# A hybrid decoder step: the last MLP unit by column groups, projection weights reloaded earlier, norm sums moved by one tile

## The reference

```python
h = rms_norm(x, norm_mix)
u = h @ w_in                        # RWKV-7 inputs, attention q/k/v/f, two merge gates
o_r, new_shift, new_wkv = rwkv_time_mix(u_r, ...)      # token shift, delta-rule state
o_f = attend(q, k, v, lf)                              # softmax with forget bias
merged = sigmoid(g_r) * (o_r @ w_br_rwkv) + sigmoid(g_f) * (o_f @ w_br_fox)
x = x + merged @ w_out
h2 = rms_norm(x, norm_ffn)
x = x + square(relu(h2 @ w_ffn_up)) @ w_ffn_down
y = rms_norm(x, norm_final)         # the outputs y_prompt and y_sample
```

## Time and profile before

| | us |
|---|---|
| median of 3 timed runs | 2189.82 |
| lowest and highest of them | 2179.16 and 2191.62 |
| the profiled execution | 2182.38 |
| its span, first to last instruction | 2180.6 |
| TensorE busy in it | 2074.7 (95%) |
| VectorE, ScalarE, GpSimd busy | 908.8, 594.1, 197.1 |
| mean granted TensorE clock | 0.986 |

### The profile page before, as it was taken

One profiled execution on the slowest core, in us unless ns is written; L12 is line 12 of the kernel. 1 busy time (PEld: TensorE's weight loads), 2 busy tenths in 40 slices (PEclk: granted clock), 3 DMA queues, 4 the chain that ended last, 5 costly groups with the idle time before them and its releaser, 6 DMA issues.

```text
span 2180.6 us, 42563 instructions
## 1 busy us (share of the span) xinstructions
PE 2074.7 (95%) x17388; PEld 1796.7 (82%) x17388; DVE 908.8 (42%) x1449; ACT 594.1 (27%) x956; POOL 197.1 (9%) x188
## 2 busy tenths in 40 slices
PE   7998899999999999998899999999999999999995
PEld 6996577777777777555566899999999999999995
DVE  6456543334444433514687654432223223222333
ACT  4014322222222222313445552332022112102212
POOL 0000112222222122001110000000000000000000
PEclk9999999999999999999999999999999999999998
DMA  3123610111121210765646461111111111111111
GB/s 145 48 78 113 214 39 22 44 44 49 49 58 49 67 42 25 184 134 188 204 150 227 147 230 63 48 43 45 48 48 39 49 48 38 48 48 40 46 38 79
DMA packets 105121, 180.96 MB, mean 83 GB/s; under 512 B 59951, under 2 KB 60271, under 8 KB 103431
## 3 DMA queue, kind: packets, MB, share of 16 engines
q1 hardware_dynamic: 102694, 170.65, 24.4%
q10 hardware_dynamic: 2304, 8.50, 1.6%
HBM read 145.58 MB, written 33.54 MB: 82 GB/s over the span
## 4 chain that ended last, share of the span: by engine, by line
PE 68%; issue 18%; POOL 4%; DVE 3%; DMA 3%; SPq 2%; ACT 2%; ACTq 0%; POOLq 0%; DVEq 0%
PE ps L289 40%; PE ps L369 13%; PE ps L941 3%; POOL arena L2113 3%; PE ps L942 3%; DMA weights<-in_wu 1%; SPq L758 1%; DMA normed<-in_vp 1%; PE ps L1123 1%; DVE arena L1893 1%; DMA normed<-in_kp 1%; PE ps L1060 1%; DVE arena L1912 1%; PE ps L1257 1%; PE ps L1182 1%
## 5 line engine op out<-in xcount | busy, mean ns | idle before, releaser
L369 PE MATMUL ps<-normed,weights 128*128 128x350 f32 x1344 | 429.9, 468 | 1.0 <-DVE arena L1686 1.0
L369 PEld LDWEIGHTS ps<-normed,weights 128*128 128x128 f32 x1344 | 246.0, 190 | 127.3 <-issue 6.8
L289 PE MATMUL ps<-h_high,wb_split 128*128 128x350 f32 x1536 | 290.5, 324 | 0.0
L289 PE MATMUL ps<-ff_high,wb_split 128*128 128x350 f32 x1536 | 290.0, 323 | 0.0
L299 ACT CAST wb_split<-weights 128x1024 fp32r<-128x1024 f32 x88 | 92.1, 1047 | 599.0 <-PE ps L289 590.9
L289 PEld LDWEIGHTS ps<-ff_high,wb_split 128*128 128x128 f32 x1536 | 255.2, 189 | 0.0
L289 PEld LDWEIGHTS ps<-h_high,wb_split 128*128 128x128 f32 x1536 | 254.7, 189 | 0.4
L2051 DVE TENSOR_TENSOR arena<-arena,ps 128x1050 f32 (+1 forms) x40 | 49.9, 1248 | 321.7 <-PE ps L289 321.7
L2113 POOL TENSOR_TENSOR arena<-arena,constants 64x512 f32<-64x512 f32 x120 | 132.5, 1104 | 406.4 <-DVE arena L1743 344.9
L941 PEld LDWEIGHTS ps<-arena 64*64 64x64 f32 x2400 | 145.0, 135 | 26.5 <-issue 26.1
L289 PE MATMUL ps<-ff_low,wb_split 128*128 128x350 f32 x768 | 165.5, 323 | 0.0
(11 more groups left out here) (291 smaller groups left out, 2895.2 us busy)
## 6 DMA issues: line engine op xcount, KB each, us to landing
weights<-in_wu SPq DMA_DIRECT2D x122, 512.0 KB, 3.5
normed<-in_vp SPq DMA_DIRECT2D x64, 260.0 KB, 4.6
normed<-in_kp SPq DMA_DIRECT2D x64, 256.0 KB, 5.4
arena<-chunk_dram SPq DMA_DIRECT2D x10, 1248.0 KB, 6.9
arena<-gate_dram SPq DMA_DIRECT2D x16, 525.0 KB, 3.9
chunk_dram<-arena SPq DMA_DIRECT2D x12, 520.0 KB, 4.0
chunk_dram<-fox SPq DMA_DIRECT2D x12, 520.0 KB, 3.8
arena<-samp_dram SPq DMA_DIRECT2D x10, 512.0 KB, 10.9
```

What stands on the lines that cost most here:

```text
L289: last = pe.matmul(PS[:, 3 * s + g, 0:G], ws[s][wh][:, k * P:(k + 1) * P], tile_of(x[xh], k)[:, g * G:(g + 1) * G], start=(k == 0 and wh + ...
L369: last = self.pe.matmul(PS[:, 6 + m % 2, 0:G], W[:, s, k * P:(k + 1) * P], HT[:, k, g * G:(g + 1) * G], start=(k == 0), stop=(k == KT - 1))
```

## The change

Four edits, all in the order of work:

1. `load_pairs` (pairs 1 to 7, input projection) waits for the split of the weights that it overwrites, in place of the end of the unit that uses them.
2. The norm sums of norm 0 are issued at tile 6 instead of tile 7: groups 0 and 1 before unit 1's half of tile 6, group 2 behind it.
3. The last unit (pair `PAIRS - 1`, slot 1) is run one column group after the other, 24 matmuls each into one bank, and everything behind it is per group: the add (`end_add`), the square (`end_square`), the sum in two matmuls (the running sum of seven squares, and the eighth square: `pe_end_sum`), Ln, Exp, and the multiply by gain and scale for 8 tiles (`end_normed`). Group 2's matmuls are issued in two halves between the sums.
4. GpSimd and the gain scaling on ScalarE have no part in the end; VectorE multiplies all 8 tiles, 350 columns at a time. SyncE stores twelve pieces, two tiles of one group each (128 x 2 rows of 1400 bytes).

```diff
             def load_pairs(v0, v1):
                 with sp.Fori(v0, v1) as v:
-                    load_w(v, 0)
-                    load_w(v, 1)
+                    for s in range(2):
+                        sp.wait_ge(w_split[s], v)
+                        load_w(v, s, wait=False)
...
-            for k in (0, 1, 6, 2, 3, 7, 4, 5):
-                if k < N_DVE:
-                    sp.wait_ge(h_ready, 2 * KT + k + 1)
-                else:
-                    sp.wait_ge(out_made, k - N_DVE + 1)
-                sp.dma_start(A["o_y"][:, k, :], HT[:, k, :]).then_inc(out_stored, 16)
+            for g in range(NG):
+                for j in range(KT // 2):
+                    sp.wait_ge(out_made, KT * g + 2 * j + 2)
+                    sp.dma_start(A["o_y"][:, 2 * j:2 * j + 2, g * G:(g + 1) * G],
+                                 HT[:, 2 * j:2 * j + 2, g * G:(g + 1) * G]).then_inc(out_stored, 16)
...
                 first_tile(k, 0)
-                if k == KT - 1:
+                if k == KT - 2:
                     pe.wait_ge(consts_in, 64)
                     pe_norm(pe, 0, (0, 1))
                 first_tile(k, 1)
-            pe_norm(pe, 0, (2,))
+                if k == KT - 2:
+                    pe_norm(pe, 0, (2,))
...
+            pe_down(FF_CH - 1, KT // 2 - 1)
+            pe_unit_split(pe, PAIRS - 1, 0, FS, of=BRO)
+
+            def pe_end(g, k0, k1):
+                ws = WSB[1]
+                for k in range(k0, k1):
+                    for wh, xh in ((0, 0), (0, 1), (1, 0)):
+                        last = pe.matmul(PS[:, NG + g, 0:G], ws[wh][:, k * P:(k + 1) * P],
+                                         FS[xh][:, k, g * G:(g + 1) * G], start=(k == 0 and wh + xh == 0),
+                                         stop=(k == KT - 1 and wh == 1))
+                if k1 == KT:
+                    last.then_inc(end_done, 1)
+
+            def pe_end_sum(g):
+                pe.wait_ge(sq_added, 3 * KT - 1)
+                at = slice(g * G, (g + 1) * G)
+                pe.matmul(PS[:, g, 0:G], ones, norms[2][1][:, at], start=True, stop=False)
+                pe.wait_ge(end_squared, g + 1)
+                pe.matmul(PS[:, g, 0:G], ones, norms[2][0][:, 1, at], start=False, stop=True)\
+                  .then_inc(ssum_ready[2], 1)
+
+            pe.wait_ge(w_split[1], PAIRS - PV_FILL)
+            pe.wait_ge(evac[1], PAIRS - 1 - PV_FILL)
+            pe_end(0, 0, KT)
+            pe_end(1, 0, KT)
             pe.wait_ge(evac[0], PAIRS - PV_FILL)
-            pe_norm(pe, 2)
+            pe_end_sum(0)
+            pe_end(2, 0, KT // 2)
+            pe_end_sum(1)
+            pe_end(2, KT // 2, KT)
+            pe_end_sum(2)
...
+            def end_square(g):
+                act.wait_ge(end_added, g + 1)
+                act.activation(sums[:, g * G:(g + 1) * G], XT[:, KT - 1, g * G:(g + 1) * G], ACT.Square)\
+                   .then_inc(end_squared, 1)
...
+            end_square(0)
+            end_square(1)
+            end_log(0)
+            end_exp(0, 1)
+            end_log(1)
+            end_square(2)
+            end_exp(1, 3)
+            end_log(2)
+            end_exp(2, 5)
...
-            dve_rms(dve, 2)
-            for k in range(N_DVE):
-                normed(dve, 2, k, V_NL, HT[:, k, :]).then_inc(h_ready, 1)
+
+            def end_add(g):
+                part = XT[:, KT - 1, g * G:(g + 1) * G]
+                dve.wait_ge(end_done, g + 1)
+                dve.tensor_tensor(part, part, PS[:, NG + g, 0:G], ALU.add).then_inc(end_added, 1)
+
+            def end_normed(g, count, tiles):
+                at = slice(g * G, (g + 1) * G)
+                dve.wait_ge(rms_ready[2], count)
+                for k in tiles:
+                    if k == KT - 1:
+                        dve.wait_ge(end_added, g + 1)
+                    dve.scalar_tensor_tensor(HT[:, k, at], XT[:, k, at], par[:, V_NL + k:V_NL + k + 1],
+                                             norms[2][2][:, at], ALU.mult, ALU.mult).then_inc(out_made, 1)
+
+            end_add(0)
+            end_add(1)
+            end_normed(0, 2, range(KT // 2))
+            end_add(2)
+            end_normed(0, 2, range(KT // 2, KT))
+            end_normed(1, 4, range(KT))
+            end_normed(2, 6, range(KT))
...
-            pool.wait_ge(rms_ready[2], NG + 1)
-            for k in range(N_DVE, KT):
-                pool.wait_ge(out_scaled, k - N_DVE + 1)
-                pool.tensor_tensor(HT[:, k, :], XT[:, k, :], norms[2][2], ALU.mult).then_inc(out_made, 1)
```

More of the change, by code:

```diff
@@ L58 @@
 RW_T = 14
-N_DVE = 6
 SCALE = HD ** -0.5
@@ L236, in build @@
         w_hi, w_split = [sem("w_hi0"), sem("w_hi1")], [sem("w_split0"), sem("w_split1")]
-        h_hi, out_scaled, out_made = sem("h_hi"), sem("out_scaled"), sem("out_made")
+        h_hi, out_made = sem("h_hi"), sem("out_made")
+        end_done, end_added, end_squared = sem("end_done"), sem("end_added"), sem("end_squared")
         norms = []
@@ L804, in _ @@
                     reload(v, s)
[L805 to L810 removed]
+            for g in range(NG):
[3 more added lines that the diff above has]
+                                 HT[:, 2 * j:2 * j + 2, g * G:(g + 1) * G]).then_inc(out_stored, 16)
             sp.wait_ge(kv_stored, 16)
             sp.wait_ge(sp_stored, 16)
[L813 removed]
+            sp.wait_ge(out_stored, 16 * (2 + NG * KT // 2))
         @block.tensor
@@ L1308, in pe_up, with pe_down @@
                 pe_unit_split(pe, KT * c + j + V_FF0, 1, HS)
-            def pe_down(c):
+            def pe_down(c, pairs=KT // 2):
                 v0 = KT * c + (V_FF0 + KT // 2)
@@ L1314, in pe_down @@
                 pe_unit_split(pe, v0, 1, FS)
-                with pe.Fori(1, KT // 2) as j:
+                with pe.Fori(1, pairs) as j:
                     pe_unit_split(pe, j + v0, 0, FS)
@@ L1321, in _ @@
             pe_down(0)
-            with pe.Fori(1, FF_CH) as c:
+            with pe.Fori(1, FF_CH - 1) as c:
                 with pe.Fori(0, KT // 2) as j:
@@ L1325, in _ @@
                 pe_down(c)
-            pe.wait_ge(evac[0], PAIRS - PV_FILL)
-            pe_norm(pe, 2)
+            with pe.Fori(0, KT // 2) as j:
+                pe_up(FF_CH - 1, j)
+            pe_down(FF_CH - 1, KT // 2 - 1)
[20 more added lines that the diff above has]
+            pe_end(1, 0, KT)
+            pe.wait_ge(evac[0], PAIRS - PV_FILL)
+            pe_end_sum(0)
[3 more added lines that the diff above has]
+            pe_end_sum(2)
         @block.scalar
@@ L1599, in _, with end_log, end_exp @@
                     v = PAIRS - KT // 2 + j
+                    if 2 * j + s == KT - 1:
+                        break
                     act.wait_ge(evac[s], v + 1 - PV_FILL)
                     act_square(act, 2, 2 * j + s, s)
[L1602 to L1606, removed]
                     if v + 1 < PAIRS:
                         act_split(act, v + 1, s)
-            act_rms(act, 2)
+            sums, rstd = norms[2][0][:, 1], norms[2][2]
+            def end_square(g):
+                act.wait_ge(end_added, g + 1)
+                act.activation(sums[:, g * G:(g + 1) * G], XT[:, KT - 1, g * G:(g + 1) * G], ACT.Square)\
+                   .then_inc(end_squared, 1)
+            def end_log(g):
+                act.wait_ge(ssum_ready[2], g + 1)
+                act.activation(rstd[:, g * G:(g + 1) * G], norm_out(2, g), ACT.Ln, scale=1.0 / D,
+                               bias=par[:, V_EPS:V_EPS + 1]).then_inc(rms_ready[2], 1)
+            def end_exp(g, count):
+                act.wait_ge(rms_ready[2], count)
+                part = rstd[:, g * G:(g + 1) * G]
+                act.activation(part, part, ACT.Exp, scale=-0.5).then_inc(rms_ready[2], 1)
+            end_square(0)
[7 more added lines that the diff above has]
+            end_exp(2, 5)
         @block.vector
```

## The result

| | before | after |
|---|---|---|
| median of 8 runs each, us | 2185.3 | 2166.31 |
| lowest to highest | 2178.03 to 2191.62 | 2162.34 to 2177.94 |
| ratio, 95% interval | | 0.9924, 0.9905 to 0.9943 |
| profiled execution | 2182.38 | 2169.08 |
| its span | 2180.6 | 2167.1 |

The ratio makes it 16.6 us faster (12.5 to 20.8). The forecast was 2166.

The account below looks back on a forecast made before the run. TensorE fully busy in the MLP; gains only where it idles, in projection and tail. 2.9 + 2.0 + 3.7 + 11.6 = 20.2 us, off the 2185.7 mean gives 2165.5, forecast 2166; range 2153 to 2178.

Parts of the forecast that it names:

- The tail: After the last pair's first unit: column groups let multiplies and stores start earlier, span ends 11.6 us sooner (10.4 to 12.5).
- rival 5: Last unit: 24 matmuls in a row into one PSUM bank take twice 0.161 us each; 2176 us, chance 0.03.
- GpSimd's company: Old tail: beside GpSimd's two multiplies, VectorE took 6.6 us for two of its own; that goes.
- rival 2: Tail: each of six Ln/Exp table switches also drains the engine, costing 1.28 us once more; 2172 us, chance 0.04.
- Part 1: Input projection: norm sums one tile sooner, so TensorE resumes for the second pair at 39.2, gaining 2.9 us.
- The weights for the second pair were not late before: Input projection: second-pair weights did not delay TensorE before; with the earlier reload they come far earlier still.
- The clock: Start of second pair: full clock holds over the 2.9 us pause, so 15 matmuls take 2.4, not 4.4; gain 2.0 us.
- Rival 1: Second pair: the clock falls in the 2.9 us pause all the same; gain 18.2 us, 2168 us, chance 0.18.
- the held pause of 2.5 us at 1193 us: Trace of before, 1193.1 to 1195.6 us: the clock held over this pause, 0.4 us shorter than the new one.
- Part 2: Late input projection: weights reloaded once split, so TensorE's three stops for the key sums' evacuation go; gain 3.7 us.
- Rival 3: Projection: squares late at tile 6, or VectorE's key sums still late; gain 14 to 17 us, 2170 us, chance 0.12.
- Rival 4: Tail: stores in 1400-byte rows crawl, 2.8 us each at 130 GB/s, making it slower than before; chance 0.02.

Follow-up runs that it names:

- whole_again: The changed kernel run again unaltered, on the same chip as its separate parts; 2163.35 us, ratio 0.9902 to the kernel before.
- part3_alone: The kernel before with only the last unit run by column groups (changed kernel without its reload and norm-sum edits); 2173.62 us, ratio 0.9961.
- whole_third: The changed kernel run once more unaltered, beside its version with sums at tile 5 and early table load; 2164.66 us, ratio 0.9906.
- warm_pause: The changed kernel with four extra norm-sum matmuls, result unread, on TensorE in the pause before the second pair; 2163.7 us, ratio 0.9916.
- sums_at_tile5: The changed kernel with the norm sums issued another tile sooner, at tile 5; 2162.04 us, ratio 0.9901 to the kernel before.
- vector_alone: The kernel before with all eight final multiplies on VectorE, no GpSimd or ScalarE gain scaling, stores in order; 2180.1 us, ratio 0.9985.
- no_table_switch: The changed kernel with Identity and Square for Ln and Exp in the last norm, so no table loads (output scale wrong); 2167.56 us, one run.
- part2_alone: The kernel before with only the earlier reload of the projection weights, once split; 2180.41 us, ratio 0.9984.
- early_load: The changed kernel with a one-column Ln behind the first square of the tail, loading the table early; 2163.91 us, ratio 0.9909 to the kernel before.
- part1_alone: The kernel before with only the norm sums moved from tile 7 to tile 6; 2181.71 us, ratio 0.9991.
- tile5_and_early_load: The changed kernel with norm sums at tile 5 and the early one-column Ln together; 2160.78 us, ratio 0.9896 to the kernel before.

## Why the prediction was right, step by step

The forecast of 2166 and the median of 2166.31 agree better than either is known. The result's ratio gives a gain of 12.5 to 20.8 us, whole_again's 17.9 to 24.7, and the sum of the terms was 20.2. That the last digits meet is luck; the terms are what can be judged.

**The tail, 11.6 us predicted, 10.95 measured** (10.8 between the means of three profiles with the old tail, 39.61, and of six with the new one unaltered, 28.84: after, part3_alone, whole_again, whole_third, warm_pause, sums_at_tile5). The chain was worked out to start VectorE's multiplies at E + 12.45, and the last sixteen at E + 17.35; measured 12.46 and 17.33. Sixteen took 7.99 us, 0.50 each against 0.49. The stores' rate, which no row of before showed, was taken as 1.0 us for 358 KB; at 347 GB/s it is 1.03. The queues were full from E + 19.6 instead of 19.2 and to E + 27.6 instead of 27.15, and the end of the span came 1.4 instead of 1.2 us behind: together the 0.65 us by which this term was too large. The adds of groups 0 and 1 start 3.84 us apart (2141.96 and 2145.80), so 24 matmuls into one bank take the 0.16 us each of a unit, and rival 5 is out.

What the prediction didn't see is how the gain divides. It named GpSimd's company as a part of the cost; vector_alone shows that 4.0 of the 10.8 us come from dropping it (with the gain scaling and the old store order), with no column groups at all. The other 6.8 are left for the group order.

**Table switches, rival 2: false.** Six loads of 1.28 us, each operation 0.01 us behind its load, multiplies at the predicted time. The Trainium skill ("ScalarE: Activation LUTs", What ACT_TABLE_LOAD costs) puts a drain of about 1.38 us on each switch. The trace shows the load and no drain, and no_table_switch bounds everything that all six cost the end at 1.0 to 1.2 us.

**Part 1, 2.9 us predicted, 1.96 in the result's two profiles, 2.8 in the means.** The chain from the sums to the resumption was 9.2 us in both, as the step says. The difference is in when TensorE's tiles came to the sums: 30.96 after, and 31.24 and 30.22 in two other executions with the same code, where 32.94 before less 2.9 is 30.0. The first matmuls of a run take twice the later 0.161 us, and executions spent unlike times in that. In the windows of the start, before and then after, the clock column says 1.00 all the same; what tells is the number of matmuls, the first count:

```profile
9.60:17.00 7.40, 7.32 (x37) 7.32 (x38) 7.40 (x8) 7.40 (x8) 0.00 (x0) 1.00 1.03 420
```

```profile
9.60:17.00 7.40, 6.96 (x31) 6.96 (x32) 7.40 (x8) 7.40 (x8) 0.00 (x0) 1.00 1.03 419
```

Six matmuls fewer by 17.0 us are the missing 1.0 us. The step itself was right. The mean resumption of three profiles with the old front (before, part3_alone, vector_alone) is 42.82 us, or 42.71 with part2_alone; of five with the new one (after, whole_again, whole_third, early_load, no_table_switch) it is 40.05. The sentence "The weights for the second pair were not late before" holds too: they had 2.5 us in hand. What it leaves out is that the moved sums alone would use that up, as part1_alone shows. The prediction had part 2 beside it, so the sum was not touched.

**The clock, 2.0 us predicted: the term that was mis-sized.** Rival 1 held more often than the forecast. In four of the five profiles with the new front the clock outlasted the pause of 2.9 us but fell about 1.5 us after TensorE was busy again, for some 3.4 us. In the fifth (whole_again) it didn't. The fall costs 1.5 us on the spot: from 41 to 47 us there are 30 matmuls in the profile after and 39 in that of warm_pause, nine of 0.161 us. From the resumption to the chunk stage it is 203.5 to 203.8 us in the four with the fall and 200.2, 200.5, 200.5 and 201.9 in the four executions without it (whole_again, warm_pause, tile5_and_early_load, sums_at_tile5); what goes beyond 1.5 us lies further on, where the clock's mean from 150 to 241 us is 0.94 against 0.96 to 0.98. So 0.5 of the 2.0 us came in the result's pair, and some 1.5 to 3.3 were left there. The step's argument, that a clock still full 3.3 us after the halt would survive a shorter halt, reads the fall as an effect of the idle engine at that moment. The rows after show that it can come once the engine works again, and part1_alone that it can come 2.0 us after a halt: the time for which one execution's clock outlasted a halt says little of the next. The prediction's own comparison, the held pause of 2.5 us at 1193 us, did not decide this. That short pauses keep the clock rests on three executions (0.56, 1.15, 1.15 us), where one of five kept it over 2.9 us.

**Part 2, 3.7 us predicted, 4.0 measured** (207.50 to 203.50 us between the result's two profiles, in which the half us of the clock is contained; 3.9 in part2_alone, with the old front). Waits and places were as worked out; the three stops went whole.

**Rival 3** (parts 1 and 2 give only one gain) didn't come true: the chunk stage starts at 250.8 in the mean of the three old fronts and at 243.05 in that of the five new ones, 7.7 us sooner, of 8.6 predicted. In part1_alone it did in part: the moved sums need the earlier weights, and keep 1.1 of their 2.9 us without them. **Rival 4** is out as well: 1400-byte rows moved at 347 to 355 GB/s, where 130 was the point of decision.

**What stays open.** Between the chunk stage and the MLP the same instructions took 1075.3 to 1084.6 us in the thirteen profiles. By the mean clock of that stage, TensorE was at half clock there for 27 us in the profile of before and 55 in the one of after. The 3.4 us of the result's pair were lost in one place. Between these two instructions of VectorE, 20 apart, it is 22.7 us before and 29.0 after, 6.3 more; the rest of the stage was 2.8 us sooner.

```profile
1195.27 1.80 DVE L1912 TENSOR_SCALAR arena<-arena 104x624 f32<-104x624 f32 x4
...
1217.98 1.22 DVE L303 TENSOR_TENSOR wb_split<-weights,wb_split 128x1024 fp32r<-128x1024 f32 x1
```

```profile
1185.89 1.80 DVE L1967 TENSOR_SCALAR arena<-arena 104x624 f32<-104x624 f32 x4
...
1214.85 1.22 DVE L303 TENSOR_TENSOR wb_split<-weights,wb_split 128x1024 fp32r<-128x1024 f32 x1
```

The clock's mean between them is 1.00 before and 0.66 after: a stretch at half clock lies there. The window of the kernel after shows it (0.74), and that of warm_pause, about the same place of the program, shows full clock and more matmuls done:

```profile
1196.00:1222.00 26.00, 24.49 (x187) 22.75 (x186) 16.70 (x22) 16.60 (x19) 0.00 (x0) 0.74 0.24 82
```

```profile
1188.00:1214.00 26.00, 22.82 (x246) 20.33 (x240) 16.46 (x22) 17.41 (x21) 0.00 (x0) 1.00 0.24 83
```

The same twenty instructions take 29.0, 27.7 and 28.6 us in the three profiles of the changed kernel, and 21.8 to 25.0 in the ten of all other kernels, those of early_load and no_table_switch among them, whose code is the same up to there. So the long stretch came in every profile of this one program and in no other, at 4 to 6 us. It isn't shown to be a price of the four edits, and what triggers it was not found. With the means of the profiles of a kind (7.7 at the front, 10.8 in the tail, and a middle stage of 1081.5 us in five against 1078.8 in three, 2.7 lost) it is 15.8 us, against the 16.6 by the result's ratio.

## What to carry to other kernels

When a chain is made shorter, look at what arrives second: part 1 alone kept about 1 us of 2.9, since the load of the weights waited for a unit that its own edit delays. Two engines at one elementwise job can be slower than one: time the job with one engine before dividing it. Once work is cut into groups so that the stores can start early, the stores' rate bounds the end, and a cheaper step ahead of them (here the table loads, 7.7 us in all) is worth only what it brings until the queues are full (1.0 to 1.2 us).

## What the runs showed of the hardware

- The clock can fall after a pause and not in it. With a pause of 2.9 us it fell in four of five executions, about 1.5 us after TensorE had work again (mean 0.53 from 41.5 to 45.1 us, close to the lower level of 1.2 GHz). With pauses of 1.15 us (two executions) and 0.56 us (one) it held. It can also fall 2.0 us into a pause (part1_alone).
- Where the sums come in the first unit varied by over a microsecond between executions of one code (30.96 and 31.24 us; 30.22 with extra work only behind them), with TensorE starting at 10.04, 10.12 and 9.93 us. The first matmuls run at half pace, and for unlike times: up to 17.0 us 37 were done in the profile of before, 31 in that of after and 27 in that of part1_alone.
- Beside two GpSimd multiplies two VectorE multiplies took 6.6 us; alone eight took 9.87, 1.23 each. Dropping GpSimd, the gain scaling and the old store order made the tail 4.0 us shorter.
- Stores in rows of 1400 bytes moved at 347 to 355 GB/s over windows of 8 and 10 us, in rows of 4200 bytes at 405 to 408.
- A switch between Ln and Exp cost 1.28 us, and the next operation began 0.01 us behind the load.
